# Transposes of both attentions moved from TensorE to VectorE's 32x32 blocks and SBUF-to-SBUF transfers

## What is computed

```python
h = rmsnorm(x, g_pre)
proj = h @ w_in        # split into q_a k_a v_a lr_a z_a  q_b k_b v_b z_b  m_a m_b
log_a = log_sigmoid(lr_a @ w_decay_up + b_decay_up) / 16
# branch A, 4 heads, chunks of 64: for every chunk
b = cumsum(log_a);  k_dec = k * exp(b_last - b)
S = S * exp(b_last) + k_dec^T v;  o = (q * DK**-0.5) S      # DK = 128, DV = 256
o_a = rmsnorm(o, g_gla) * silu(z_a);  y_a = o_a @ w_branch_gla
# branch B, 16 heads of 64, 2 kv heads: rope, keys of this chunk and the one before, a sink per head
p = softmax([q k^T / 8, sink]);  o_b = (p v) * silu(z_b);  y_b = o_b @ w_branch_swa
out = (sigmoid(m_a + b_a) * y_a + sigmoid(m_b + b_b) * y_b) @ w_out
x = x + rmsnorm(out, g_post)
```

## Time and profile before

| | |
|---|---|
| median of 3 runs | 1950.27 us (1947.94 to 1950.64) |
| span of the profiled execution | 1944.9 us |
| TensorE busy, matmuls | 1902.9 us, 98% |
| VectorE, ScalarE, GpSimd busy | 66%, 44%, 51% |
| transfers on SyncE's queue | 386.94 MB, 61.3% of 16 engines' time |
| granted clock of TensorE | 0.9 or more in tenths of full speed, all slices but the last |

### The profile page before, as it was taken

How to read it: one execution, slowest core, us unless ns; L and a number is a source line. 1 busy time by engine, 2 the same in 40 slices (tenths; PEclk the granted TensorE clock), 3 DMA queues, 4 the chain that set the end, 5 groups by cost and what they waited for, 6 DMA issues and landing times.

```text
span 1944.9 us, 29064 instructions
## 1 busy us (share of the span) xinstructions
PE 1902.9 (98%) x9936; PEld 1527.0 (79%) x9936; DVE 1288.5 (66%) x2140; ACT 851.5 (44%) x1888; POOL 985.2 (51%) x640
## 2 busy tenths in 40 slices
PE   8999999999999999999999999999999999999996
PEld 7878877777777778887888777777777777887885
DVE  6868876976766667547578866655666557546265
ACT  5467364543344453313267354543443453225431
POOL 4534454455333347625434555554333357538955
PEclk9999999999999999999999999999999999999998
DMA  7524375577666677885733444545676686775873
GB/s 277 156 75 152 102 241 177 183 233 222 207 216 212 218 233 257 281 293 191 265 92 114 145 152 154 158 147 160 203 227 222 194 284 232 249 229 193 276 253 121
DMA packets 269157, 388.79 MB, mean 200 GB/s; under 512 B 32275, under 2 KB 157779, under 8 KB 255699
## 3 DMA queue, kind: packets, MB, share of 16 engines
q1 hardware_dynamic: 269011, 386.94, 61.3%
HBM read 254.28 MB, written 132.58 MB: 199 GB/s over the span
## 4 chain that ended last, share of the span: by engine, by line
PE 46%; DVE 3%; issue 1%; DMA 1%; POOL 1%; ACT 0%; SPq 0%; POOLq 0%; DVEq 0%; ACTq 0%
PE pu L954 30%; PE pu L955 11%; PE pm L955 4%; PE pm L1138 1%; DMA kw_s<-kb_d 0%; DVE a_lo L1580 0%; POOL keep L2039 0%; POOL w_lo L1974 0%; PE pm L1163 0%; DMA d_g<-dw_d 0%; POOL a_lo L1983 0%; DMA qb_d<-ct 0%; DVE keep L1958 0%; PE pm L1193 0%; PE pm L1161 0%
## 5 line engine op out<-in xcount | busy, mean ns | idle before, releaser
L954 PE MATMUL pu<-a_hi,w_hi 128*128 128x512 f32 x1824 | 720.8, 397 | 13.2 <-DVE u L1814 4.1
L954 PE MATMUL pu<-a_hi,w_lo 128*128 128x512 f32 x1824 | 707.2, 390 | 0.6 <-POOL w_lo L1974 0.6
L954 PE MATMUL pu<-a_lo,w_hi 128*128 128x512 f32 x1824 | 706.4, 390 | 0.0
L1974 POOL TENSOR_TENSOR w_lo<-t,w_hi 128x512 fp32r<-128x512 f32 x256 | 356.7, 1402 | 479.5 <-ACT w_hi L1304 479.5
L1974 POOL TENSOR_TENSOR w_lo<-w_raw,w_hi 128x512 fp32r<-128x512 f32 x264 | 398.4, 1520 | 320.6 <-ACT w_hi L1304 320.5
L954 PEld LDWEIGHTS pu<-a_hi,w_hi 128*128 128x128 f32 x1824 | 342.2, 188 | 99.8 <-issue 30.8
L954 PEld LDWEIGHTS pu<-a_hi,w_lo 128*128 128x128 f32 x1824 | 342.3, 188 | 74.0 <-POOL w_lo L1974 1.0
L954 PEld LDWEIGHTS pu<-a_lo,w_hi 128*128 128x128 f32 x1824 | 342.8, 188 | 66.9
L1304 ACT ACTIVATE w_hi<-t 128x512 fp32r<-128x512 f32 x256 | 158.7, 629 | 326.3 <-DVE t L515 256.1
L955 PE MATMUL pu<-a_hi,w_hi 128*128 128x512 f32 x544 | 212.2, 390 | 0.0
L955 PE MATMUL pu<-a_hi,w_lo 128*128 128x512 f32 x544 | 211.7, 389 | 0.0
(11 more groups left out here) (185 smaller groups left out, 2393.8 us busy)
## 6 DMA issues: line engine op xcount, KB each, us to landing
w_raw<-in_w SPq DMA_DIRECT2D x81, 1024.0 KB, 6.7
va_d<-ct SPq DMA_DIRECT2D x32, 256.0 KB
qb_d<-ct SPq DMA_DIRECT2D x32, 256.0 KB
zb_d<-ct SPq DMA_DIRECT2D x32, 256.0 KB
q_s<-qb_d SPq DMA_DIRECT2D x32, 256.0 KB, 3.5
z_s<-zb_d SPq DMA_DIRECT2D x32, 256.0 KB, 3.1
gb_d<-gb SPq DMA_DIRECT2D x32, 256.0 KB, 3.3
za_d<-ct SPq DMA_DIRECT2D x32, 256.0 KB
```

Of the source, the lines that this page charges most:

```text
L954: return nc.tensor.matmul(dst, weights, moving, start=start, stop=stop, skip_group_check=True)
L1974: TT(flat(w_lo[o.n % NWB][:, :, :]), src, as_f32(flat(w_hi[o.n % NWB][:, :, :])), ALU.subtract) \
```

## The change

TensorE no longer transposes for either attention. A 128x128 transpose becomes two steps. VectorE's `transpose` turns each 32x32 block in its place, in one instruction over the whole tile. Then SyncE issues sixteen transfers from SBUF to SBUF (`turn_blocks`), each of which moves 32 partitions of one block column to the partitions and the place of the turned block: 32 rows of 1 KB each for the probabilities, 512 bytes each for `o_n`. `prob`, `prob_t`, `o_n` and the new `o_t` are laid out in blocks of 32 for that.

k and v need no second step: `ka_d` and `va_d` are now stored in blocks of 32 tokens by 32 channels (`TB` = 32), by four transfers a tile instead of one, in rows of 128 bytes; a job's load then brings the block rows to the partitions of their tokens, and VectorE's block transpose in place finishes it. `kd` and `vt` are gone; `k_g` and `v_g` serve for them.

The matmuls with `ind` are gone. `later` has the sum over the whole chunk in the column of each chunk's last token; that row of `dw` is stored to `total_d`, a row of ones stands in its place in `dw_d`, and `decay_s` is loaded from `total_d`, turned by its access, at r = 72 (`TOTALS`). A transfer of 128 rows of `dw` becomes two of 63 rows and two of one.

The steps move: turn of the probabilities VectorE r+4, SyncE r+5, `prob_values` still r+8; in `GLA` state on VectorE r+3, `state_reads` r+6, `o_n` scaled at r+7, turned at r+8 and r+9, multiplied into `ga` at r+13, stored at r+14. GpSimd multiplies z by the gain at r+12. q has a load and a semaphore of its own. The first gate loads for `yB` are issued two slots later. ScalarE's copies to `prob_t` and `vt` are gone.

```diff
+def stores_of(g, n):
+
+    return P // TB if g.kind == "v" or (g.kind == "qk" and n % 2) else 1
+
+
+def stores_before(n, m):
+
+    return 16 * sum(stores_of(GROUPS[k], n) for k in STORED if k < m)
...
-    ka_d = spill("ka_d", [HEADS_A * DK, SEQ])
-    va_d = spill("va_d", [D, SEQ])
+    ka_d = spill("ka_d", [SEQ // TB, TB, HEADS_A * DK // TB, TB])
+    va_d = spill("va_d", [SEQ // TB, TB, D // TB, TB])
...
-        k_g = [tile(f"k_g{n}", [P, 2, P], f32, m + 5 * K1 * n + K1) for n in range(2)]
-        v_g = [tile(f"v_g{n}", [P, 4, P], f32, m + 5 * K1 * n + 2 * K1) for n in range(2)]
+        k_g = [tile(f"k_g{n}", [P, 2 * DK], f32, m + 5 * K1 * n + K1) for n in range(2)]
+        v_g = [tile(f"v_g{n}", [P, 2 * DV], f32, m + 5 * K1 * n + 2 * K1) for n in range(2)]
...
+                elif g.kind == "v" or (g.kind == "qk" and n % 2):
+                    dst, first = (va_d, e * (P // TB)) if g.kind == "v" else (ka_d, g.idx * (DK // TB))
+                    for q in range(P // TB):
+                        go(dst[tok.start // TB:tok.stop // TB, :, first + q, :].rearrange("j d t -> d j t"),
+                           ct[n][q * TB:(q + 1) * TB, :].rearrange("p (j t) -> p j t", t=TB), ct_out[n])
...
+                go(k_g[b][:, :], ka_d[tg, :, pr * 8:(pr + 1) * 8, :].rearrange("j d g t -> (j d) (g t)"), gla_in[b])
+                go(v_g[b][:, :], va_d[tg, :, pr * 16:(pr + 1) * 16, :].rearrange("j d g t -> (j d) (g t)"), gla_in[b])
...
+            def turn_blocks(dst, src, done):
+
+                for j in range(P // TB):
+                    for i in range(P // TB):
+                        go(dst[j * TB:(j + 1) * TB, i, :, :], src[i * TB:(i + 1) * TB, j, :, :], done)
...
+                    for c in range(2):
+                        rows, last = slice(c * CH, (c + 1) * CH - 1), (c + 1) * CH - 1
+                        go(dw_d[t0 + rows.start:t0 + rows.stop, :], dw[t % 2][rows, :], dw_out[t % 2])
+                        go(total_d[t0 // CH + c:t0 // CH + c + 1, :], dw[t % 2][last:last + 1, :], dw_out[t % 2])
...
+                if r - 5 in SWA:
+                    n = 16 * sb + SWA[r - 5]
+                    sp.wait_ge(pt_ok, n + 1)
+                    sp.wait_ge(pv_ok, n)
+                    turn_blocks(prob_t, prob[n % 2], prob_out[n % 2])
+                if r == TOTALS:
+                    for d in dw_out:
+                        sp.wait_ge(d, 16 * 4 * NT // 2 * (sb + 1))
+                    sp.wait_ge(st_ok, 16 * sb)
+                    for h in range(HEADS_A):
+                        src = total_d[sb * SB // CH:(sb + 1) * SB // CH, h * DK:(h + 1) * DK]
+                        with nc.allow_non_contiguous_dma(reason="decay of whole chunks by columns"):
+                            go(decay_s[:, h, :, :].rearrange("p t c -> p (t c)"), src.rearrange("n p -> p n"), total_in)
...
+                if r - 9 in GLA:
+                    n = 16 * sb + GLA[r - 9]
+                    sp.wait_ge(o_t_ok, n + 1)
+                    sp.wait_ge(ga_ok, n)
+                    turn_blocks(o_t, o_n, o_t_in)
+                if r - 10 in GLA:
+                    load_gla_z(sb, GLA[r - 10])
...
-                    ins = mm(pm[b][:, 2 * h:2 * h + 2], log_a[b][:, h * DK:(h + 1) * DK], cs["ind"])
...
-            def prob_transposes(n):
-                pe.wait_ge(p_ok, n + 1)
...
+            def prob_values(n):
+                pe.wait_ge(prob_out[n % 2], 16 * PT_DMAS * (n // 2 + 1))
+                pe.wait_ge(swa_v_in[n % 2], (n // 2 + 1) * 16 * 2)
+                pe.wait_ge(gb_ok, n)
+                for c in range(2):
+                    for par in range(2):
+                        o = pm[4][par * HD:(par + 1) * HD, :].rearrange("p (e c i q) -> p c i e q", e=4, c=2, i=2)
+                        ins = mm(o[:, c, :, :, :], v_s[n % 2][:, c, :],
+                                 prob_t[:, 2 * c:2 * c + 2, par * 4:(par + 1) * 4, :])
...
-            def key_transposes(n):
-                pe.wait_ge(gla_in[n % 2], (n // 2 + 1) * 16 * 4)
-                if n:
-                    pe.wait_ge(kd_ok, n)
-                    pe.wait_ge(vt_ok, n)
-                for h in range(2):
-                    tr(pm[0][:, h * P:(h + 1) * P], k_g[n % 2][:, h, :], ident[:, :])
-                for e in range(4):
-                    ins = tr(pm[1][:, e * P:(e + 1) * P], v_g[n % 2][:, e, :], ident[:, :])
-                ins.then_inc(tr_ok, 1)
...
+                pe.wait_ge(kd_ok, 2 * n + 2)
+                pe.wait_ge(st_ok, n)
...
-            def out_transposes(n):
-                pe.wait_ge(o_n_ok, n + 1)
-                pe.wait_ge(st_ok, min(n + 2, 16 * (n // 16 + 1)))
-                for e in range(4):
-                    ins = tr(pm[2][:, e * P:(e + 1) * P], o_n[:, e, :], ident[:, :])
-                ins.then_inc(ot_ok, 1)
...
+                if r - 6 in GLA:
+                    state_reads(16 * sb + GLA[r - 6])
...
-                    A(flat(prob_t[:, 0:4, :]), pm[2][:, :], ACT.Copy).then_inc(pt_a_ok, 1)
...
-                    A(vt[:, :], pm[1][:, :], ACT.Copy).then_inc(vt_ok, 1)
...
+                if r - 7 in GLA:
+                    n = 16 * sb + GLA[r - 7]
                     act.wait_ge(o_r_ok, n + 1)
+                    act.wait_ge(o_t_in, 16 * PT_DMAS * n)
...
+                    p = prob[n % 2]
+                    dve.wait_ge(p_ok, n + 1)
+                    V.transpose(blocks(p), blocks(p)).then_inc(pt_ok, 1)
...
+                if r - 8 in GLA:
+                    n = 16 * sb + GLA[r - 8]
+                    dve.wait_ge(o_n_ok, n + 1)
+                    V.transpose(blocks(o_n), blocks(o_n)).then_inc(o_t_ok, 1)
...
+                    dve.wait_ge(gla_in[b], (n // 2 + 1) * 16 * 3)
+                    V.transpose(v_g[b][:, :], v_g[b][:, :]).then_inc(kd_ok, 1)
+                    link(V.transpose(k_g[b][:, :], k_g[b][:, :]))
+                    TT(k_g[b][:, :], k_g[b][:, :], d_g[b][:, :], ALU.mult).then_inc(kd_ok, 1)
...
+                if r - 13 in GLA:
+                    n = 16 * sb + GLA[r - 13]
+                    dve.wait_ge(o_t_in, 16 * PT_DMAS * (n + 1))
+                    dve.wait_ge(zg_ok, n + 1)
                     dve.wait_ge(ga_out, 16 * n)
-                    dve.wait_ge(gb_out, 16 * 16 * (sb + 1))
-                    for e in range(4):
-                        ins = STT(ga[:, e, :], pm[2][:, e * P:(e + 1) * P], gate_g[:, 4 * pr + e:4 * pr + e + 1],
-                                  z_g[:, e, :], ALU.mult, ALU.mult)
-                    ins.then_inc(ga_ok, 1)
+                    TT(ga[:, :, :].rearrange("p e (j t) -> p e j t", t=TB),
+                       o_t[:, :, :, :].rearrange("p j e t -> p e j t"),
+                       z_g[:, :, :].rearrange("p e (j t) -> p e j t", t=TB), ALU.mult).then_inc(ga_ok, 1)
...
+                if r - 12 in GLA:
+                    n = 16 * sb + GLA[r - 12]
+                    pr = n % 16 // NT
+                    pool.wait_ge(gla_z_in, 16 * (n + 1))
+                    TT(z_g[:, :, :], z_g[:, :, :], gate_g[:, 4 * pr:4 * pr + 4].unsqueeze(2).broadcast_to([P, 4, P]),
+                       ALU.mult).then_inc(zg_ok, 1)
...
+    later = same & ((r[:, None] > r[None, :]) | (r[None, :] % CH == CH - 1))
```

More of the change, by code:

```diff
@@ L235, in two_pi_parts @@
     return parts + [float(np.float32(rest))]
-COLS = dict(gpre=8, ggla=8, bmerge=16, gpost=8, inv_freq=1, half_pi=1, one=1, ind=2, ones=2, sinks=16)
+COLS = dict(gpre=8, ggla=8, bmerge=16, gpost=8, inv_freq=1, half_pi=1, one=1, ones=2, sinks=16)
 NCOLS = sum(COLS.values())
@@ L428, in build @@
         gla_in = [sem(f"gla_in{n}") for n in range(2)]
+        gla_q_in = [sem(f"gla_q_in{n}") for n in range(2)]
+        prob_out = [sem(f"prob_out{n}") for n in range(2)]
+        o_t_in, total_in = sem("o_t_in"), sem("total_in")
         gla_z_in = sem("gla_z_in")
@@ L1099, in decay_sums @@
                 for k, part in enumerate((la_hi, la_lo)):
[L1100 to L1102 removed]
+                    ins = mm(pm[4][:, :], blob[:, LATER0:NBLOB], part[b][:, :], start=k == 0, stop=k == 1)
                 ins.then_inc(sf_ok, 1)
@@ L2092 @@
                  inv_freq=np.tile(inv_freq, 4)[:, None], half_pi=np.full((P, 1), np.pi / 2),
-                 one=np.ones((P, 1)), ind=ind, ones=np.ones((P, 2)), sinks=np.broadcast_to(sinks, (P, 16)))
+                 one=np.ones((P, 1)), ones=np.ones((P, 2)), sinks=np.broadcast_to(sinks, (P, 16)))
     cols = np.concatenate([np.asarray(parts[name], np.float32).reshape(P, width) for name, width in COLS.items()],
@@ L2096 @@
     r = np.arange(P)
-    later = (r[:, None] > r[None, :]) & (r[:, None] // CH == r[None, :] // CH)
+    same = r[:, None] // CH == r[None, :] // CH
+    later = same & ((r[:, None] > r[None, :]) | (r[None, :] % CH == CH - 1))
     x0 = np.ascontiguousarray(np.asarray(x)[0])
```

209 lines of the change are left out of this document (85 added, 124 removed).

## The result

The changed kernel takes 2322.65 us (median of 4 runs, 2317.94 to 2327.91) against 1950.08 before (four runs; the table above has three of them): a ratio of 1.1916, with a 95% interval of 1.1897 to 1.1935. That is slower, outside the range of 1890 to 2060, and also slower than rival C's 2110. It was to be 0.6% slower, and slower at all with a chance of 0.54. The profiled execution has a span of 2316.1 us.

The account below looks back on a forecast made before the run. TensorE bounds the kernel now; SyncE was to end last or draw level in attention. Span 1944.9 - 13 + 26 + 3 - 10 + 6 = 1957 us, with 5.4 added 1962 in the median; range 1890 to 2060.

Parts of the forecast that it names:

- rival C: SyncE's transfers cost as `kw_s`, 0.64 us each, so SyncE alone sets each attention period: span 2110; chance 0.15.
- The bound before: Whole kernel: TensorE, busy in 98% of the span, sets the time; whatever leaves it shortens the span if nothing replaces it.
- what leaves TensorE: Transposes of probabilities 27.2 us, of outputs, k and v 37.1, chunk sums 13.0: together 77.3 us off TensorE.
- The price of an issue: SyncE's sixteen transfers a job at 0.465 us each, taken from the rope table loads: 7.4 us a job.
- the sign of C: In the profile after, SyncE issues of 0.6 us would show the forecast wrong.
- The other issues: SyncE's remaining issues a job: window block 0, 15.3 at 0.56 us; block 1, 12.5 at 0.50; linear, 10.9 at 0.54.
- The chain: Window attention: transfers plus landing take 9.8 to 10.6 us against 9.4 of cover; TensorE stands about 1 us a job.
- the loop: Linear attention: transfers, landing, copy, transpose and `ga` take 12.8 us from job to job, under 13.3 of SyncE.
- Linear attention: Both linear stretches: 13.9 us a job, 0.3 under now, so -10 us over 32 jobs.
- VectorE's block transpose: Window attention: VectorE's copy from PSUM becomes a block transpose of twice the elements, taken as 1.2 us.
- Handover to the gates: End of attention: last jobs run into the later gate loads, 0 to 8 us each time, taken as 3, 6 in all.
- The totals' loads: Eight loads of 4-byte pieces, due some 65 slots later: nothing, or 5 us a block if they hold up SyncE.

Follow-up runs that it names:

- `same`: Series of sixteen SBUF-to-SBUF transfers that stay on their partitions, in a program with the layer left out: 0.63 us of the queue each.
- `wide`: Series of SBUF-to-SBUF transfers of 128 partitions of 256 bytes, two or three dimensions, in a program with the layer left out: 0.63 us each.
- `half`: Series of SBUF-to-SBUF transfers of 64 partitions, in a program with the layer left out: 0.63 us of the queue each.
- the small program: Only series of sixteen or thirty-two transfers, the layer left out: 0.46 us each for 32 partitions with one side in HBM, 0.63 between SBUF tiles.

## Why the prediction was wrong, point by point

- **The bound before, and what leaves TensorE (77.3 us): held, where it could be seen.** Window attention of block 1 with one transfer gives back 12.9 of 13.6. The chunk sums are the exception: of 13.0, start to start, 6.5 fall to each block; TensorE's busy time fell by 5.3 in block 0, and 3.8 of them came back as waits, most for VectorE.
- **The price of an issue: the step that failed.** "The nearest row is the eight loads of the rope tables", 0.465. They have one side in HBM; the transfer of the change has none. It costs 0.63 alone and 0.64 in the kernel: 16 come to 10.1 us a job, not 7.4. Rival C had this price (10.2), for another reason: it was put on 64 partitions, and the series `same`, `wide` and `half` show that partitions don't matter between two tiles. At 0.15 it was held too unlikely; no row of the trace had both sides in SBUF, and the choice between two rows of loads from HBM was made by the partition count. The prediction named this as what would bring it down, another price than a load of 32 partitions, and 0.6 us as the sign of C.
- **The price alone isn't enough.** With it, C's sum gives a span of 2110, and the profile has 2316.1. Of these 206 us, 89 fall to linear attention, 53 and 27 to window attention of block 1 and block 0, 28 to the handovers, 7 to the chunk sums. The next points say what each is.
- **The other issues: mis-sized too.** Window attention of block 0 was to have 15.3 a job at 0.56, 8.6 us. It has 230 in 16 jobs, 14.4, and they cost 0.675 + 0.043 each, 10.3 us; block 1 has its 12.5, at 0.611 + 0.043, 8.2 us in place of 6.2. The medians of the earlier trace rows left out the long ones (maxima of 1.1 to 1.6 us there): before, the mean of all issues in that stretch of block 0 was 0.544 + 0.043 already. Of the 155 us that the 230 take after, 31 go to the 45 stores of k and v and 9 to the four loads of the totals. It isn't the full queue, for the most part, that makes them dear there: with one transfer a job, the queue at 0.73 of the stretch, the mean is 0.651. The count was good, the price wasn't. With 9.6 for the sixteen (240 issues fall in the stretch, 15 jobs' worth, spread over 16), that is the 20.0 us which SyncE needs in block 0, against the prediction's 16.0 and C's 18.8.
- **The chain: right in kind, small in size.** TensorE was to stand "about 1 us a job" at the values; it stands 5.2. The chain of 7.4 + 2.4 to 3.2 is 10.1 + 1.9. The slack of 9.4 was counted by TensorE's slots, but the issues don't start when VectorE is done: they start when SyncE comes to them, behind the job's other issues. Cutting the loop on three engines gives 71 us, 33 of them in window attention, whose stretches had lost 191; there the queue's sum is most of the loss.
- **Linear attention: "-10" was +152.** The loop was put at 12.8 us under 13.3 of issues. The issues came to 15.5 and 14.4 us a job (279 and 259 over 18), and the period to 18.7 and 18.1. Here the queue isn't full (0.83, 0.80), and with the loop cut on three engines only 4.5 and 13.4 us went. The loop by its parts, with the medians of the trace, is 10.1 + 1.8 (landing) + 0.8 + 0.7 + 1.7 (`ga`, put at 0.7) = 15.1 us, so it doesn't fill the period by itself either. The prediction's loop went through ScalarE's copy to `o_n`, and the added stands of ScalarE were to be "some 3 us"; ScalarE's longest wait in block 0's stretch (us in total, times, longest):

```profile
ACT o_n L1460 <- DMA o_t<-o_n: 100.6, 15, 14.1
```

  6.7 us a job. In block 1 it is 100.3, and SyncE itself stands 26.4 and 31.6 us for the job before at `ga`. No run took ScalarE's wait away, and with half of the issues on ScalarE's queue the stretches kept 323.3 and 314.5 us. That the count of issues costs the time here too is shown by four transfers a job (256.5 and 253.1 us); by which wait it does so is open.
- **VectorE's block transpose: held.** "I take 1.2" for 128x1024; in the kernel with one transfer, 1.235:

```profile
L1747 DVE STREAM_TRANSPOSE prob<-prob 128x1024 f32<-128x1024 f32 x16 | 19.8, 1235 | 0.5 <-POOL prob L2052 0.5
```

  Of 128x512 it takes 0.67 to 0.71 and of 128x256 0.40 us. But its cover was counted too well: the kernel with one transfer misses about 15 us in linear attention of block 0, with VectorE busy 0.79 of the stretch and `ct` among the waits. That the 4 us a job that were called free weren't free at each point is my reading; no run shows it apart.
- **Handover to the gates: 3 us each was 20 and 14.** With four transfers a job it is 6 and 3, with one 3 and 2, so it goes with the number of issues; that the queue comes out of the attention with its work behind it is the likely reason, and wasn't tested.
- **The totals' loads: "nothing, or 5 us a block".** 2.9 us in block 0, nothing that can be seen in block 1.
- **The clock** wasn't in the prediction, and in window attention the idle matmuls say that it needn't have been.

What stays open beside the linear stretches: why four transfers a job lose 9 us more in window attention of block 0 than one (240.0 and 231.4 us), while the issues are only 2 us a job apart.

## What to carry over

When work is moved to DMA, add up the issuing queue of a whole stretch: every issue that is there already by its mean (not its median), the new ones by a row with the same ends (HBM or SBUF on each side) and the same shape, and compare it with the stretch; a queue that needs more than the period sets it, however idle the DMA engines are (they were at 0.52 to 0.60 here). A queue that needs less is no proof of the contrary: the linear stretches lost 152 us with the queue at 0.80 to 0.83, so the chain through the transfers has to be added up by itself, with every engine that waits for a landing. Where there is no such row, measure the price in a program of a few lines first: it would have told 0.63 from 0.465 in one run. And take a change of several parts apart: the part that moves k and v is worth 0.7%, and was hidden under the part that cost 19%.

## What the runs showed of the hardware

- A transfer between two SBUF tiles takes 0.59 to 0.60 us of SyncE's or ScalarE's queue, one of 32 partitions with an end in HBM 0.42 us, each with 0.043 us to the next. From HBM the shape does matter: 16 loads of 64 rows of 768 bytes took 0.597 us each in the same program, which is the price of `kw_s`, and 16 of 128 rows of 256 bytes 0.432. Between SBUF tiles neither partitions (32 to 128) nor the length of the rows (256 bytes to 4 KB) nor size decided it, up to the 128 KB transfers of the kernel with four (median 0.601 us). Single ones, behind other kinds of transfers, had a shorter median and the same mean: 0.495 and 0.599 us for the 512 KB of the kernel with one. Size isn't free in every case: the eight stores of 1 MB to HBM at the end of the small program took 1.24 us each in the median. From GpSimd's queue a series of fifteen took 7.46 us, 0.50 each.
- Four loads whose pieces are 4 bytes held the queue for 9.54 us, 2.4 each.
- Behind a wait of 3.41 us the granted clock was 0.50 through the values matmuls that followed and 1.00 in the 2 us from 1459.00 on; over all jobs such matmuls took 634 ns in the median, 379 where idle matmuls had gone before.
